# Attention of a two-layer trunk: eight instead of six of ten key tiles split into a high and a low part, two of the low parts made by DVE

## The reference, cut to what matters

```
def block_attention(q, k, v):
    ...
    def one_block(qblk):
        s = jnp.einsum('bqkgd,bskd->bkgqs', qblk, k).astype(F32)
        p = jax.nn.softmax(s, axis=-1).astype(v.dtype)
        return jnp.einsum('bkgqs,bskd->bqkgd', p, v)
```

## Time and profile before

| What | us |
|---|---|
| three runs, median (lowest to highest) | 3104.09 (3102.58 to 3104.70) |
| the profiled execution, its own time | 3103.27 |
| the span of its trace | 3101.5 |
| attention stage in the trace, from the first turned scores to the last product | 549.55 to 806.56 |
| a latent batch, most of them | 15.00 |

### The profile page before, as it was taken

One profiled execution on the slowest core, in us unless ns is written; L12 is line 12 of the kernel. 1 busy time (PEld: TensorE's weight loads), 2 busy tenths in 40 slices (PEclk: granted clock), 3 DMA queues, 4 the chain that ended last, 5 costly groups with the idle time before them and its releaser, 6 DMA issues.

```text
span 3101.5 us, 41472 instructions
## 1 busy us (share of the span) xinstructions
PE 2917.8 (94%) x16141; PEld 2504.6 (81%) x16141; DVE 2031.2 (65%) x2488; ACT 1238.6 (40%) x2055; POOL 1426.6 (46%) x1002
## 2 busy tenths in 40 slices
PE   7999988999899999999999999989799999999998
PEld 3898876666689999978877887768689999978877
DVE  3679776554568444587877376578778544488886
ACT  2311164676543222233324477544353332333322
POOL 1121064666434444487851121176433443488870
PEclk9999998999999999999999999966799999999999
DMA  5566574000222323333243323241232323332241
GB/s 207 175 211 221 194 213 148 24 1 28 85 82 79 115 88 113 107 115 116 98 137 98 109 93 135 78 133 54 67 107 74 104 95 108 125 123 74 100 176 61
DMA packets 230880, 346.81 MB, mean 112 GB/s; under 512 B 32118, under 2 KB 124318, under 8 KB 230686
## 3 DMA queue, kind: packets, MB, share of 16 engines
q1 hardware_dynamic: 230686, 344.17, 33.2%
HBM read 259.18 MB, written 84.94 MB: 111 GB/s over the span
## 4 chain that ended last, share of the span: by engine, by line
PE 66%; POOL 12%; DVE 9%; issue 5%; ACT 4%; DMA 2%; SPq 1%; PEldq 0%; POOLq 0%; ACTq 0%; DVEq 0%; PEld 0%
PE psum L1002 19%; PE psum L1194 9%; POOL d_slot L1134 6%; PE psum L662 6%; PE psum L2950 5%; PE psum L1299 3%; PE psum L1647 3%; PE psum L665 3%; PE psum L1176 2%; PE psum L3964 2%; PE psum L439 2%; PE psum L2609 1%; DVE ada_acc L296 1%; PE psum L829 1%; PE psum L2590 1%
## 5 line engine op out<-in xcount | busy, mean ns | idle before, releaser
L1194 PE MATMUL psum<-d_slot 128*128 128x512 f32 x2016 | 468.1, 392 | 8.6 <-DVE yacc L1239 3.7
L1194 PEld LDWEIGHTS psum<-d_slot 128*128 128x128 f32 x2016 | 379.7, 189 | 92.9 <-DVE yacc L1239 5.3
L1002 PE MATMUL psum<-AT,w_slot 128*128 128x288 f32 x2688 | 369.1, 296 | 4.7 <-POOL w_slot L967 4.7
L1002 PEld LDWEIGHTS psum<-AT,w_slot 128*128 128x128 f32 x2688 | 362.6, 189 | 5.1 <-POOL w_slot L967 5.1
L1134 POOL TENSOR_TENSOR d_slot<-down_a,d_slot 128x512 fp32r<-128x512 f32 x168 | 300.1, 1810 | 72.2 <-ACT d_slot L1125 72.0
L591 POOL TENSOR_TENSOR WT<-RAW,WT 128x1024 fp32r<-128x1024 f32 (+3 forms) x30 | 111.1, 3726 | 429.5 <-ACT WT L580 429.5
L662 PE MATMUL psum<-WT,AT 128*128 128x512 f32 (+1 forms) x1296 | 282.5, 378 | 4.0 <-ACT stage L717 4.0
L1002 PE MATMUL psum<-s_hi,w_slot 128*128 128x288 f32 x1344 | 269.0, 295 | 3.3 <-issue 1.7
L662 PEld LDWEIGHTS psum<-WT,AT 128*128 128x128 f32 x1296 | 231.7, 190 | 46.8 <-ACT stage L717 4.3
L967 POOL TENSOR_TENSOR w_slot<-RAW,w_slot 128x512 fp32r<-128x512 f32 x112 | 155.8, 1402 | 224.1 <-ACT w_slot L963 224.1
L1002 PEld LDWEIGHTS psum<-s_hi,w_slot 128*128 128x128 f32 x1344 | 215.3, 188 | 4.1 <-issue 2.1
(11 more groups left out here) (467 smaller groups left out, 6083.6 us busy)
## 6 DMA issues: line engine op xcount, KB each, us to landing
RAW<-ffn_w SPq DMA_DIRECT2D x40, 1024.0 KB, 6.6
ada_raw<-ada_w SPq DMA_DIRECT2D x36, 1024.0 KB, 6.2
hidden<-hid SPq DMA_DIRECT2D x56, 576.0 KB, 3.1
down_a<-hidden SPq DMA_DIRECT2D x48, 512.0 KB, 5.9
RAW<-ffn_w SPq DMA_DIRECT2D x48, 512.0 KB, 7.4
RAW<-w_in_even SPq DMA_DIRECT2D x5, 2048.0 KB, 8.2
RAW<-w_in_odd SPq DMA_DIRECT2D x5, 2048.0 KB, 7.9
mix_x<-x_all SPq DMA_DIRECT2D x18, 512.0 KB, 3.3
```

What stands on the lines that cost most here:

```text
L1002: mm = nc.tensor.matmul(psum[:, bank + b, 0:HB], w_slot[p][:, w, k, :], TOKENS[p][x][:, k, b * HB:(b + 1) * HB], start=(begins and k == 0 ...
L1194: mm = nc.tensor.matmul(psum[:, D_RING[q % 3] + pair % 2, :], slot[:, 0, x, k, pair * P:(pair + 1) * P], slot[:, 1, w, k, :], start=(k == ...
```

## The change

Key tiles 1 and 6 become split ones too, so that eight of ten are (0, 1, 2, 3, 5, 6, 7, 8) and two whole (4, 9). Their low parts are made by DVE, by a subtraction that stands between two maxima; POOL keeps the six low parts it had, in the place they had. DVE's low parts have a semaphore of their own, for which PE waits. The values have eight high-and-low tiles and three plain ones (with the context's) in the memory in which they had six and five, and the early gates move from there into columns of AT, the tile of the mixer's output, that are written later, as four pieces of 128 columns; a row buffer of the modulation (`col_row_late`) moves too.

```diff
-        row_at = AT0 + 4 * KD * T - 4 * K
+        row_at = AT0
...
-        values_1 = attT("values_1", [P, KT - 5, KV, P])
-        values_hl = attT("values_hl", [P, 6, KV, P + HD], F32R)
-        mo_early = attT("mo_early", [P, 2, 4, P])
+        values_1 = attT("values_1", [P, 3, KV, P])
+        values_hl = attT("values_hl", [P, KT - 2, KV, P + HD], F32R)
+        mo_early = [Region(at, at + 4 * 4 * T)(f"mo_early{n}", [P, 4, T]) for n, at in enumerate((AT0, AT0 + 4 * KD * T))]
...
-        SPLIT = [kt for kt in range(KT) if kt % 5 in (0, 2, 3)]
+        SPLIT = [kt for kt in range(KT) if kt % 5 != 4]
+        DVE_SPLIT = [1, 6]
+        POOL_SPLIT = [kt for kt in SPLIT if kt not in DVE_SPLIT]
...
-                    pe.wait_ge(low_done, splits_to(s) + 1)
+                    pe.wait_ge(low_done_dve if kt in DVE_SPLIT else low_done, lows_to(s) + 1)
...
+            def low(n, kt):
+                if key_tiles(n) == 1:
+                    return
+                s = steps_to(n) + kt
+                j = splits_to(s)
+                dve.wait_ge(exp_done, s + 1)
+                if j >= 2:
+                    dve.wait_ge(pv_done, SPLIT_STEPS[j - 2] + 1)
+                nc.vector.tensor_tensor(p_low[:, j % 2, :], prob[:, s % 3, :], p_high[:].bitcast(F32)[:, j % 2, :], ALU.subtract).then_inc(low_done_dve, 1)
+
...
                     biggest(n, 0)
+                    low(n - 1, 1)
                     biggest(n, 1)
                     if n >= 2:
                         out(n - 2)
                     biggest(n, 2)
+                    low(n - 1, 6)
                     biggest(n, 3)
...
-                    for kt in SPLIT[:3]:
+                    for kt in POOL_SPLIT[:3]:
...
-            return mo_early[:, t, :, :] if is_early(l, t) else by_head(mo_x[t % 2])
+            return mo_early[t][:, :, CTX * P:T] if is_early(l, t) else by_head(mo_x[t % 2])
```

More of the change, by code:

```diff
@@ L2487, in trunk @@
         late_sems = Stage(2)
-        late_sems.set = stage_sets[2][0:9] + stage_sets[2][15:]
+        late_sems.set = stage_sets[2][0:9] + stage_sets[2][15:] + stage_sets[1][29:30]
         late_of = late_sems
-        score_done, max_done, m_turned, m_kept, q_copied, st_done, exp_done, pv_done, inv_done, out_ready, att_high, att_low, v_laid, low_done = (
+        score_done, max_done, m_turned, m_kept, q_copied, st_done, exp_done, pv_done, inv_done, out_ready, att_high, att_low, v_laid, low_done, low_done_dve = (
             late_of(n) for n in ("score_done", "max_done", "m_turned", "m_kept", "q_copied", "st_done", "exp_done", "pv_done", "inv_done",
-                             "out_ready", "att_high", "att_low", "v_laid", "low_done"))
+                             "out_ready", "att_high", "att_low", "v_laid", "low_done", "low_done_dve"))
         PARTS = [(0, 512), (512, 512), (1024, 256)]
@@ L2535, in splits_to, with lows_to @@
             return sum(1 for r in SPLIT_STEPS if r < s)
+        def lows_to(s):
+            of = DVE_SPLIT if step_of(s)[1] in DVE_SPLIT else POOL_SPLIT
+            return sum(1 for r in SPLIT_STEPS if r < s and step_of(r)[1] in of)
         def m_slot(n):
@@ L2750, in att_vector @@
                 keep_maxima(n)
+                if n // 2 == CTX:
+                    low(n - 1, 6)
                 if n == LAST - 1:
@@ L2787, in att_gpsimd @@
             copy_queries(1)
-            for kt in SPLIT:
+            for kt in POOL_SPLIT:
                 low(kt)
@@ L2805, in att_gpsimd @@
                 if key_tiles(n - 1) > 1:
-                    for kt in SPLIT[3:]:
+                    for kt in POOL_SPLIT[3:]:
                         low(steps_to(n - 1) + kt)
@@ L2835, in gate_in @@
         def gate_in(l, t):
-            return mo_early[:, t, :, :] if is_early(l, t) else by_head(mo_x[t % 2])
+            return mo_early[t][:, :, CTX * P:T] if is_early(l, t) else by_head(mo_x[t % 2])
         def gate_of(l, t):
-            return mo_early[:, t, :, :] if is_early(l, t) else by_head(mo_s[t % 2])
+            return mo_early[t][:, :, CTX * P:T] if is_early(l, t) else by_head(mo_s[t % 2])
         def squares_of(l, t):
```

## The result

| | us |
|---|---|
| changed kernel, median of 4 runs (lowest to highest) | 3124.62 (3119.98 to 3126.26) |
| kernel before, runs beside it | 3104.11 (3102.58 to 3104.70) |
| ratio, with its 95% interval | 1.0067 (1.0055 to 1.0079) |
| profiled execution of the changed kernel: time, span, mean granted clock | 3119.98, 3118.2, 0.960 |

The change makes the kernel slower by 0.67%, 20.5 us. In the two profiled executions it is 16.7 us. The changed kernel's profiled execution is the fastest of its four runs, so no trace shows the 3.8 us between 16.7 and 20.5. The next table says where the 16.7 lie. I read it from the starts of the products that turn the maxima (L2575 before, L2582 after): one stands at the end of each batch.

The account below looks back on a forecast made before the run. PE bounds the clean batches, and p_high of key tile 3 sets the time in six heavy ones. 3.5 + 5.8 + 2.9 + 7.2 = 19.4 us on 3103.27 gives 3122.7, forecast as 3123 us, range 3106 to 3130.

Parts of the forecast that it names:

- The slot's wait: On ACT, p_high of key tile 3 waits for key tile 1's product to free its slot, starting 0.77 us later.
- x + 1.70: Forecast start of p_high of key tile 3 on ACT; x is the start of its L2591 on PE.
- PE's gain: Rounded products replace fp32 ones for two key tiles on PE: 0.30 us saved a batch, 4.8 in all 16.
- A clean batch: Latent batch without weight quarter or gate product: PE's gain less new waits, taken as +0.35 us; ten give +3.5.
- The SBUF access: DVE and POOL take turns at SBUF; DVE's low part of 6 delays `low` of 5 by 0.57 in heavy batches.
- The heavy batches: Four batches with weight quarter L2802, two with a gate product: PE waits 2.92 and 1.84 us; +5.8 and +2.9.
- The clock: PE's granted clock falls behind long waits in four L2802 batches and one gate batch: +7.2 us, upper bound 10.
- The end of the stage: Last latent batch, context, up to the output projection: counted only as the tenth clean batch, +0.35 us.
- The first rival (PE's gain stands): p_high of key tile 3 need not wait, PE's 4.8 us gain remains: 3098.5, or 3102 with DVE's part; 15%.
- The rival of DVE's low parts: DVE's low parts of key tiles 1 and 6 are late everywhere and hold PE: 8 us more, 3131; 8%.
- The rival of a clock that stays up: All forecast terms except the clock's falls behind PE's waits in the heavy batches: 3115.5 us; 17%.

Follow-up runs that it names:

- the run with the wait alone: Kernel before, with only p_high of key tiles 3 and 7 also waiting for the product two key tiles back: 3121.46 us, ratio 1.0057.
- three slots: Changed kernel with a third slot for the rounded exponential p_high, low parts keeping two: 3110.06 us, ratio 1.0016.
- the run with POOL's new order on the kernel before: Kernel before, with POOL's weight quarters and gate products queued behind the low parts of key tiles 5, 7 and 8: 3095.87 us, ratio 0.9980.
- the run with the moved gates: Kernel before, with only the early gates and the row buffer in their new places in memory: 3101.06 us, ratio 0.9993.
- the run with all repairs: Changed kernel with a third p_high slot, POOL's weights and gate products behind the low parts, DVE's squares behind the context's maximum: 3099.49 us, ratio 0.9981.

## Why the prediction was right, step by step

- **The slot's wait** was forecast at x + 1.70 and measured at x + 1.71, and the run with the wait alone shows that it is the cause, not a companion.
- **PE's gain** of 0.30 a batch was measured as 0.32 with three slots. That it would be eaten up was right; even with three slots the batches keep 0.2 of it at four places and nothing at four others.
- **A clean batch** was taken at +0.35 and is +0.51. The delay at key tile 2, 0.2, was called covered, and it is not: PE waits and restarts there, 0.19 in all, and so finds the low part of 3 ready. Key tile 5 costs 0.26 (forecast 0.23), 7 costs 0.31 (0.25) and 8 costs 0.10. Their sum, 0.86, less 0.32 is 0.54 by these starts.
- **The SBUF access.** DVE's low part of 6 took 1.16 at 638.04 and ended 0.56 behind POOL's low part, the 0.55 that I had read from the earlier trace rows. In the heavy batches it costs 0.46 instead of 0.57: without DVE's low parts the wait is 2.31 in place of 2.77. The prediction does not say how it came to 0.57; the rows that it read give 1.73 - 1.27 = 0.46. The Trainium skill ("SBUF — State Buffer", section "Who interferes with whom") states an exclusive lock between a DVE instruction with two SBUF inputs and a GpSimd instruction that reads SBUF; the 1.16 and the 0.46 agree with it.
- **The heavy batches** wait 2.77 where 2.92 was forecast, and 1.67 where it was 1.84. A batch grew by 1.44 and 1.47 in the two gate batches (1.45 forecast), where the clock held; four more at 1.46 are 5.8.
- **The clock** is the term that was wrong. The step that failed is that a wait longer than 2.48 is followed by a fall: I had expected five falls, and behind four waits of 2.76 and 2.77 and two of 1.67 there were two. 9.36 - 5.8 = 3.5 us for them is 1.75 each in the mean, where 1.45 was forecast, but they are unlike: the first two heavy batches are 2.4 us longer than twice 1.46, the last two 1.15. Another came behind the context's wait of 2.75. The wait behind the stage, 2.48 before and 2.51 now, was followed by a fall before and not now: -1.6.
- **The end of the stage** was in the sum only as the tenth clean batch, and it is 2.4 above that. In the profiled execution this and 1.3 more in the eight clean batches stand against the clock's falls that did not come, and the whole is 16.7 where 19.4 was forecast; by the medians it is 20.5. So the mechanism was right, and that the sum comes so near is in part luck: its lines in the table are off by 0.4 to 2.4 us each way, and these errors nearly cancel.

The first rival (PE's gain stands) fell at the place that I had named for it, the start of `p_high` of 3. The rival of DVE's low parts fell with the run without them; what it describes shows only with three slots, in the first batch. The rival of a clock that stays up was half right.

## What to carry to other kernels

When more steps use a buffer of fixed depth, count in steps of the program how far back the reader of the slot now lies: here the same two slots went from three or four key tiles back to three or two. For key tile 3 it is two, and that wait of 0.65 us on an engine with idle time cost the full engine more than the change saved. Before paying for a delay, look for what stands in a queue between the late step and its reader without need; POOL's weight quarters could move and gave 0.2% even without the change. When a step is moved back in one queue, move its readers in the other queues with it, or the wait moves there.

## What the runs showed of the hardware

Behind the stage PE waits for POOL ahead of the third group of products of the output projection (L2950 before, L2972 after) in all eleven profiled executions of this study, for 2.48 to 2.52 us each time. The granted clock fell to 0.50 behind five of these waits (2.48, 2.49 and three of 2.52) and stayed at 1.00 behind six (2.49, 2.50 twice, 2.51 twice and 2.52). These are the windows behind the wait in the run with POOL's new order on the kernel before, where it held.

```profile
815.00:817.00 2.00, 1.24 (x5) 1.05 (x6) 1.97 (x3) 0.00 (x0) 2.00 (x2) 1.00 0.00 0
817.00:819.00 2.00, 2.00 (x10) 1.66 (x9) 1.97 (x3) 1.92 (x5) 0.42 (x1) 1.00 0.00 0
```

And these are the windows at the same place in the run with the moved gates, where it fell, behind a wait of 2.52.

```profile
820.00:822.00 2.00, 1.24 (x4) 1.04 (x5) 1.97 (x3) 0.00 (x0) 2.00 (x2) 0.83 0.00 0
822.00:824.00 2.00, 2.00 (x6) 1.52 (x6) 1.97 (x3) 1.92 (x5) 0.40 (x1) 0.50 0.00 0
```

Up to the next landmark, the transposes of the gated rows, it takes 21.32 to 21.38 us from the first product of the projection where the clock held and 22.77 to 22.96 where it fell: 1.6 us. The length of the wait alone does not decide. At the start of the stage PE waits 1.00 to 1.01 us for DVE and soon after 0.35 in all eleven executions; in two the clock fell behind that, as this window of the run with all repairs shows, and in nine it did not.

```profile
550.00:552.00 2.00, 2.00 (x7) 1.61 (x6) 1.40 (x2) 1.08 (x2) 1.10 (x1) 0.50 0.38 95
```

For a wait like that of the projection a forecast should take such a fall at a chance, here about one in two, and not for certain. The Trainium skill ("TensorE: Matmul & The Clock Gate", section "What's actually happening") says of the clock's rise that its point varies from run to run of the same kernel. No kernel was profiled twice here, and the falls are those of different kernels at the same place; they vary too.
